# Two heads side by side on TensorE's row and column halves, and two waits moved, in a two-block transformer kernel

## The reference

```python
# first block: 4 heads of 64, keys of this and the previous chunk of 128, bias and mask, a sink in the denominator
logits = einsum('bnqhgd,bnjhd->bnhgqj', qb, kb) * dh ** -0.5
p = exp(logits - m);  probs = p / (sum(p) + exp(sink - m))
out = einsum('bnhgqj,bnjhd->bnqhgd', probs, vb)
# first block: 4 heads of 64 against 256 memory rows, plain softmax
logits = einsum('bshd,bmhd->bhsm', q, mem_k) * dh ** -0.5
# second block: 16 query heads, 4 key heads, over the keys that a top-k of an index score selects
q = rope_partial(rmsnorm(q, q_norm), pos)
logits = where(valid, einsum(q, k_sel) * HEAD_DIM ** -0.5, -inf);  o = einsum(softmax(logits), v_sel)
```

## Time and profile before

| | |
|---|---|
| runs | 1598.68, 1603.06, 1604.56 us; median 1603.06 |
| profiled execution | 1604.89 us, of which 1603.1 are the span of the core |
| PE busy | 1387.6 us, 87% of the span |
| POOL busy | 820.2 us, 51% |
| DVE busy | 640.7 us, 40% |
| ACT busy | 378.0 us, 24% |
| mean granted clock of PE | 0.943 of full |

### The profile page before, as it was taken

One profiled execution on the slowest core, in us unless ns is written; L12 is line 12 of the kernel. 1 busy time (PEld: TensorE's weight loads), 2 busy tenths in 40 slices (PEclk: granted clock), 3 DMA queues, 4 the chain that ended last, 5 costly groups with the idle time before them and its releaser, 6 DMA issues.

```text
span 1603.1 us, 18199 instructions
## 1 busy us (share of the span) xinstructions
PE 1387.6 (87%) x7092; PEld 1024.8 (64%) x7092; DVE 640.7 (40%) x937; ACT 378.0 (24%) x726; POOL 820.2 (51%) x712
## 2 busy tenths in 40 slices
PE   4898889589898589899999999959898499999993
PEld 4777777477676558878778888848776433333331
DVE  3140351424891335463778456661331411111112
ACT  3211142401221235410221544350103011111110
POOL 7678704447758430088888533548792123333320
PEclk9999989799999799999999999989998599999997
DMA  5423200132223020024321212162146069999964
GB/s 187 134 66 105 79 27 27 37 131 80 79 80 105 27 79 1 1 74 136 105 76 57 91 42 67 66 262 100 59 181 266 13 267 379 373 376 377 371 242 173
DMA packets 85235, 216.28 MB, mean 135 GB/s; under 512 B 23508, under 2 KB 32420, under 8 KB 71588
## 3 DMA queue, kind: packets, MB, share of 16 engines
q1 hardware_dynamic: 62076, 199.22, 33.7%
q0 software_dynamic: 13824, 8.44, 1.8%
q10 hardware_dynamic: 9256, 7.51, 1.4%
HBM read 255.99 MB, written 26.22 MB: 176 GB/s over the span
## 4 chain that ended last, share of the span: by engine, by line
PE 47%; PEld 14%; DVE 9%; POOL 6%; issue 6%; DMA 4%; ACT 4%; PEldq 3%; DVEq 3%; ACTq 2%; POOLq 1%; SPq 1%
PE ps L951 10%; PE ps L133 6%; PE ps L134 6%; PE ps L135 6%; PE ps L963 5%; PEld ps L133 5%; PEld ps L134 5%; PEld ps L135 5%; POOL w_lo L484 4%; POOL w_hi L481 3%; PE ps L819 2%; PE ps L723 2%; PE ps L876 2%; PE ps L943 2%; PEldq L596 1%
## 5 line engine op out<-in xcount | busy, mean ns | idle before, releaser
L481 POOL TENSOR_TENSOR w_hi<-stage,unit 128x512 fp32r<-128x512 f32 (+2 forms) x304 | 318.1, 1077 | 476.4 <-PE ps L135 439.9
L484 POOL TENSOR_TENSOR w_lo<-stage,w_hi 128x512 fp32r<-128x512 f32 (+2 forms) x304 | 403.5, 1358 | 10.8
L133 PE MATMUL ps<-hi,w_hi 128*128 128x512 f32 (+1 forms) x600 | 239.0, 398 | 40.5 <-POOL w_lo L484 26.1
L134 PE MATMUL ps<-hi,w_lo 128*128 128x512 f32 (+1 forms) x600 | 236.5, 394 | 0.0
L135 PE MATMUL ps<-lo,w_hi 128*128 128x512 f32 (+1 forms) x600 | 236.0, 393 | 0.0
L133 PE MATMUL ps<-w_hi,hi 128*128 128x512 f32 (+3 forms) x560 | 198.8, 355 | 13.8 <-POOL w_lo L484 6.6
L134 PE MATMUL ps<-w_hi,lo 128*128 128x512 f32 (+3 forms) x560 | 196.8, 351 | 0.0
L135 PE MATMUL ps<-w_lo,hi 128*128 128x512 f32 (+3 forms) x560 | 196.7, 351 | 0.0
L951 PE MATMUL ps<-w_gu,xT 128*64 128x512 f32 x768 | 171.6, 599 | 3.4 <-DMA w_gu<-w_up,over_u 2.0
L133 PEld LDWEIGHTS ps<-hi,w_hi 128*128 128x128 f32 x600 | 115.7, 193 | 70.9 <-issue 27.5
L135 PEld LDWEIGHTS ps<-lo,w_hi 128*128 128x128 f32 x600 | 115.9, 193 | 23.9
(11 more groups left out here) (407 smaller groups left out, 1798.5 us busy)
## 6 DMA issues: line engine op xcount, KB each, us to landing
stage<-w_in SPq DMA_DIRECT2D x84, 512.0 KB, 4.5
w_gu<-w_gate SPq DMA_DIRECT2D x32, 1024.0 KB, 12.4
w_gu<-w_up SPq DMA_DIRECT2D x32, 1024.0 KB, 14.6
w_dn<-w_down SPq DMA_DIRECT2D x32, 1024.0 KB, 10.7
stage<-w_out SPq DMA_DIRECT2D x16, 512.0 KB, 4.6
stage<-w_ssd_branch SPq DMA_DIRECT2D x16, 512.0 KB, 4.7
stage<-w_in SPq DMA_DIRECT2D x20, 256.0 KB, 3.1
stage<-w_attn_branch SPq DMA_DIRECT2D x8, 512.0 KB, 4.2
```

The costliest lines, as they stand in the source:

```text
L133: pe.matmul(out, x[0], w[0], start=first, stop=False)
L134: pe.matmul(out, x[1], w[0], start=False, stop=False)
L481: nc.gpsimd.tensor_tensor(w_hi[:, b, k, 0:n], stage[:, b, k, 0:n], unit[:].broadcast_to([P, n]), ALU.mult)
L484: last = nc.gpsimd.tensor_tensor(w_lo[:, b, k, 0:n], stage[:, b, k, 0:n], w_hi[:, b, k, 0:n].bitcast(F32), ALU.subtract)
```

## The change

1. **Scores.** Queries and keys lie so that head h of an even and an odd number are on the lower and the upper 64 partitions. The four products of a batch use 64 rows each, alternating between the halves (`lanes`). The key tiles need no zeros any more; their memsets go, and ACT writes each key head twice instead.
2. **Values.** The values are the stationary operand (64 columns) and the turned probabilities stream. Even heads go to PSUM partitions 0 to 63, odd heads to 64 to 127, so the result has features on the partitions at once, and the two transposes of the output go. In the second attention a product streams two heads (256 columns).
3. **Denominators.** Since queries now lie on the free axis, the reciprocals must be spread over partitions: four new products per batch (a column broadcast to 64 columns as weights, `ident` streaming) into `p_r`, an ACT copy of `p_r` to `share1` or `share2`, and DVE multiplies `p_v` by it. The reciprocal (`denominators`) is taken one step earlier.
4. **Order.** Per step PE now does the scores of i, the values of i-2, both pairs of transposes of i-1 one after the other, and the spreading product of i-1. There is one step fewer, and the projection in the last two steps comes in three pieces each.
5. **First wait.** DVE signals `sq_ready` right behind the sum of the squares (L1603) instead of behind all rounds, and ACT takes the root before `gate_a(0)`.
6. **Second wait.** SP issues the first two half tiles of `w_ssd_branch` before it waits for `ssd_done`.

```diff
@@ -420,6 +421,7 @@
                 halves(w2, 0, Z2 + 256 * i, 256)
             halves(w2, 0, Z2 + 1536)
+            halves(d["w_ssd_branch_2"][0], 0, 0)
             sp.wait_ge(ssd_done, 1)
             for i in range(7):
                 sp.wait_ge(gate_saved[i], 16)
@@ -433,7 +435,8 @@
             sp.dma_start(xres[:], x1_dram.rearrange("(t p) n -> p t n", p=P)).then_inc(x1_back, 16)
             for r in range(2):
                 for c in range(2):
-                    halves(d["w_ssd_branch_2"][0], 1024 * r, 512 * c)
+                    if (r, c) != (0, 0):
+                        halves(d["w_ssd_branch_2"][0], 1024 * r, 512 * c)
             for c in range(2):
                 halves(d["w_out_2"][0], 0, 512 * c)
             assert tiles[0] == 2 * JOBS
...
@@ -710,22 +713,18 @@
                         if i == batches:
                             pe.wait_ge(s_free, base + batches)
                             chunks = beside()
-                        for _ in range(2):
+                        for _ in range(3):
                             next(chunks)
-                    for half in range(2):
-                        b = i - 2
-                        if 0 <= b < batches:
+                    b = i - 2
+                    if 0 <= b < batches:
+                        for half in range(2):
                             pe.wait_ge(pT_ready[half], base + b + 1)
-                            if base + b > 0 and half == 0:
-                                pe.wait_ge(yt_ready, base + b)
-                            for h in (2 * half, 2 * half + 1):
-                                for kb in range(nkb(b)):
-                                    last = pe.matmul(p_v[:, HD * h:HD * (h + 1)], pT(b)[:, h, P * kb:P * (kb + 1)],
-                                                     values(b, h, kb), start=(kb == 0), stop=(kb == nkb(b) - 1))
-                            if half == 1:
-                                last.then_inc(v_full, 1)
-                        b = i - 1
-                        if 0 <= b < batches:
+                        if base + b > 0:
+                            pe.wait_ge(y_made, base + b)
+                        values(b, p_v).then_inc(v_full, 1)
+                    b = i - 1
+                    if 0 <= b < batches:
+                        for half in range(2):
                             if half == 0:
                                 pe.wait_ge(exp_ready, base + b + 1)
                             if base + b + half > 0:
@@ -735,38 +734,41 @@
                                     last = pe.transpose(p_t[:, h % 2, P * kb:P * (kb + 1)],
                                                         pr(b)[:, h, P * kb:P * (kb + 1)], ident[:])
                             last.then_inc(t_full, 1)
-                    b = i - 3
-                    if 0 <= b < batches:
-                        pe.wait_ge(yt_ready, base + b + 1)
+                        pe.wait_ge(den_ready, base + b + 1)
                         if base + b > 0:
-                            yt_free(b)
-                        for c in range(2):
-                            last = pe.transpose(p_yt[:, P * c:P * (c + 1)], yt[:, b % 2, P * c:P * (c + 1)], ident[:])
-                        last.then_inc(yt_full, 1)
+                            pe.wait_ge(share_ready, base + b)
+                        for h in range(4):
+                            lanes = slice(HD * (h % 2), HD * (h % 2 + 1))
+                            last = pe.matmul(p_r[lanes, P * (h // 2):P * (h // 2 + 1)], sm[:, 5, b % 4, h:h + 1].broadcast_to([P, HD]),
+                                             ident[:], start=True, stop=True)
+                        last.then_inc(r_full, 1)
                 pe.wait_ge(s_free, base + batches)
                 for _ in chunks if beside else ():
                     pass
-                yt_free(batches)
+                pe.wait_ge(y_made, base + batches)
...
@@ -815,16 +817,26 @@
             def scores2(b, s):
                 n, g = query_block(b), b % 4
-                for i in range(4):
-                    last = pe.matmul(s[:, i, 0:P * (n + 1)].rearrange("p (t k) -> p t k", k=P), qT2[:, 4 * (g // 2) + i, P * n:P * (n + 1)],
-                                     kT2[g % 2][g // 2][:, 0:n + 1, :], start=True, stop=True)
+                for h in range(4):
+                    lanes = slice(HD * (h % 2), HD * (h % 2 + 1))
+                    last = pe.matmul(s[:, h, 0:P * (n + 1)], qT2[lanes, 2 * g + h // 2, P * n:P * (n + 1)],
+                                     kT2[g // 2][lanes, g % 2, 0:P * (n + 1)], start=True, stop=True)
+                return last
+
+            def values2(b, out):
+                n, g = query_block(b), b % 4
+                for kb in range(n + 1):
+                    for odd in range(2):
+                        last = pe.matmul(out[HD * odd:HD * (odd + 1), 0:256].rearrange("p (c t) -> p c t", c=2),
+                                         kvt[:, kb, 256 + HD * g:256 + HD * (g + 1)], pT2[:, odd:4:2, P * kb:P * (kb + 1)],
+                                         start=(kb == 0), stop=(kb == n))
                 return last
             pe.wait_ge(kT_ready, 1)
             pe.wait_ge(qT_ready, 2)
...
+            def shares(b, base, dst):
+
+                A.wait_ge(r_full, base + b + 1)
+                if b > 1:
+                    A.wait_ge(y_made, base + b - 1)
+                A.activation(dst[:, b % 2, :], p_r[:, 0:256], ACT.Copy).then_inc(share_ready, 1)
+
...
+            A.wait_ge(sq_ready, 3)
+            A.activation(st[:, 7, 0:64], st[:, 6, 0:64], ACT.Sqrt, scale=1.0 / HD, bias=st[:, 9, 0:1]).then_inc(rms_ready, 1)
             A.wait_ge(x1_saved, 16)
             gate_a(0)
             s = turns.see()
-            for j in range(2):
-                lanes = slice(HD * j, HD * (j + 1))
-                for c in range(2):
-                    last = A.activation(kT2[j][c][lanes], ps[s][lanes, c, :].rearrange("p (t n) -> p t n", t=TT), ACT.Copy)
+            for g in range(4):
+                for odd in range(2):
+                    last = A.activation(kT2[g // 2][HD * odd:HD * (odd + 1), g % 2, :], ps[s][HD * (g % 2):HD * (g % 2 + 1), g // 2, :], ACT.Copy)
             last.then_inc(kT_ready, 1)
             A.drain().then_inc(turn_free[s], 1)
...
             gate_a(1)
-            A.wait_ge(sq_ready, 3)
-            A.activation(st[:, 7, 0:64], st[:, 6, 0:64], ACT.Sqrt, scale=1.0 / HD, bias=st[:, 9, 0:1]).then_inc(rms_ready, 1)
             A.wait_ge(gate_saved[0], 16)
             for c in range(2):
                 s = turns.see()
-
-                for j in range(2):
-                    for odd in range(2):
-                        last = A.activation(qT2[HD * j:HD * (j + 1), 4 * c + odd:4 * c + odd + 3:2, :],
-                                            ps[s][HD * odd:HD * (odd + 1), 2 * j:2 * j + 2, :], ACT.Copy, scale=HD ** -0.5)
-                last.then_inc(qT_ready, 1)
+                A.activation(qT2[:, 4 * c:4 * c + 4, :], ps[s][:], ACT.Copy, scale=HD ** -0.5).then_inc(qT_ready, 1)
                 A.drain().then_inc(turn_free[s], 1)
             s = turns.see()
             A.activation(gate_next[:], ps[s][:], ACT.Tanh, scale=0.5)
             A.drain().then_inc(turn_free[s], 1)
             A.dma_start(gates_dram[1], gate_next[:]).then_inc(gate_saved[1], 16)
-            for i in range(16 + 3):
+            for i in range(16 + 2):
                 if i < 16:
                     softmax(i, 8, P * (query_block(i) + 1), pr2[:, i % 2], pr2[:, i % 2], False)
                 if i == 1:
                     A.wait_ge(gate_saved[1], 16)
                 if 0 <= i - 1 < 16:
                     turned_probabilities(i - 1, 8, P * (query_block(i - 1) + 1), pT2)
-                b = i - 3
+                    shares(i - 1, 8, share2)
+                b = i - 2
                 if b >= 0:
-                    A.wait_ge(yt_full, 8 + b + 1)
+                    A.wait_ge(y_made, 8 + b + 1)
                     n, g = query_block(b), b % 4
                     A.activation(yah[:, 2 * g:2 * g + 2, P * n:P * (n + 1)],
-                                 p_yt[:, 0:256].rearrange("p (c t) -> p c t", c=2), ACT.Copy).then_inc(yT_ready, 1)
+                                 y2[:, b % 2, :].rearrange("p (c t) -> p c t", c=2), ACT.Copy).then_inc(yah_ready, 1)
             def into_conv(n):
...
-            def probabilities_used(b, base, yt, sinks_too):
+            def denominators(b, base, sinks_too):
                 k = b % 4
                 V.wait_ge(exp_ready, base + b + 1)
-                V.wait_ge(v_full, base + b + 1)
                 den = sm[:, 1, k, :]
                 if sinks_too:
                     V.tensor_tensor(den, den, sm[:, 4, k, :], ALU.add)
                     V.drain()
-                V.reciprocal(sm[:, 5, k, :], den)
-                V.drain()
-                V.tensor_tensor(yt[:, b % 2, :].rearrange("p (h d) -> p h d", h=4),
```

(28 more changed lines are left out.)

83 lines of the change are left out of this document (38 added, 45 removed).

## The result

Four executions of the changed kernel took 1572.22, 1574.46, 1577.99 and 1578.34 us, median 1576.22; the four of the kernel before have 1602.06 as their median. The medians lie 25.8 us apart. The ratio on record is 0.9829, with a 95% interval of 0.9801 to 0.9857; of 1602.06 us that is 27.4 us, between 22.9 and 31.9. Forecast were 1575 us, in a range from 1556 to 1591. The profiled execution has 1578.34 us, 26.6 less than that of before.

A forecast was written before the change was run, and what follows sets the result against it. PE, busy 87% of the span, bounds the kernel by its work plus its waits. Gains of 15.0 + 3 + 7 + 0.3 + 2.5 = 27.8 us take 1604.9 to 1577.1, as a median 1575.3; range 1556 to 1591.

The forecast's parts named there:

- Part 1: Early query root: 25.2 us gained at the query wait, less 8.4 new wait and 1.8 half clock: 15.0 us won.
- Part 2, second attention: Second attention: steps at 512 keys fall from 8.9 to 7.9 us; 7 us won, bounds -15 and +25.
- First attention: First attention: memory batches' period falls from 5.56 to 5.2 us; 3 us won, bounds -5 and +8.
- the step that failed: First attention's first four batches: they hang on DVE's sinks and on `lo`, which stay.
- The 0.3 us for shorter read-outs of queries and keys: Read-outs of queries and keys (L1052): 0.3 us shorter.
- Part 3: Early SSD branch weights: projection starts near 1072 instead of 1073.93, clock up earlier; 2.5 us won, bounds 0 and 8.
- the first (POOL not late): Half tile split at 492: POOL isn't late, the early root gives 25 us, total 1565; chance 0.14.
- the third (more late): Half-tile stall grows, next half tile late too, attentions give nothing; early root gives 8, total 1592; chance 0.09.
- The second, PE's own bound: Attentions reach PE's own bound; the second attention gives 25 us, total 1557; chance 0.07.
- The fourth: Attentions: pairs don't overlap in these forms; second loses 15 us, first 5, total 1605; chance 0.03.
- The fifth, the half clock through both attentions: Gaps in each step bring the half clock in both attentions; total 1648, slower; chance 0.03.

The follow-up runs named there:

- Experiment 2: The changed kernel without DVE's two products over the second block's queries, which are then only rotated: ratio 0.9782 to the kernel before.
- root_only: The kernel before with nothing but the early query root (sq_ready signalled behind the sum of squares): 1592.56 us, ratio 0.9920.
- small_readouts: The changed kernel with the second block's queries read out in eight copies of 64 partitions instead of two of 128: 1576.63 us, ratio 0.9821.
- spread_between: The changed kernel with PE's spreading product between the two pairs of transposes instead of behind them: 1568.12 us, ratio 0.9756.
- own_banks: The changed kernel with a bank of its own for each pair of turned probabilities in batches of 256 keys or fewer: 1567.67 us, ratio 0.9748.
- Experiment 4: Two runs on the changed kernel: spreading product between the transpose pairs, 1568.12 us; each pair in its own bank at 256 keys or fewer, 1567.67 us.

## Why the prediction was right

The forecast was 27.8 us against the profiled execution; 26.6 came. The mechanisms of the three parts were the right ones. That the sum comes so close is in part luck, since several terms were missed in both directions and the misses cancel.

- **Part 1, 15.0; measured 15.7.** The wait went, and the new one stands where it was put: 8.16 us against 8.4. The split of the half tile takes 18.8 us from its start against the 19.5 reckoned (481.25 to 500.7). Experiment 2 shows the cause. The projection behind the stop took 23.70 us instead of 22.04, so the restart cost 1.7 us against 1.8. Not seen as a matter of its own: the working put the new read-outs of the queries (1.88 us each) into this part. By root_only 3.6 of the 15.7 us of the trace come with the new layout, and by small_readouts 4.0 with the read-outs alone, though small_readouts is no slower in the whole time.
- **Part 2, second attention, 7; measured 7.25.** The path that bounds the step was the right one: 7.82 us at 512 keys against 7.9. By blocks 32.3, 26.6, 20.6 and 14.7 against 30.6, 27, 21.1 and 15.7; the sums are 94.2 and 94.4. Two terms were mis-sized. The opening two steps took 15.3 us instead of 13.9 and the third 9.1 instead of 7.9, with the second batch's scores at the half clock (3.46 us) and a granted clock of 0.85 over the third step; I had reckoned with less of it. Part of that is the execution's: small_readouts has 14.3 and 7.8 for the same steps. The spreading product issues in 0.59 us (580.87 to 581.46), not 0.45, between its bounds of 0.43 and 0.86: 0.074 us for each of its eight records. In its favour the steps at 256 and 128 keys are 4.82 and 3.4 to 3.6, not 5.05 and 3.7.
- **First attention, 3; measured 2.3.** The memory step fell further than I thought, to 4.71 and not 5.2: the chain over scores, maxima and exponentials lost the scores' half and nothing was added to it, since the copy lies beside the exponentials. But the sliding batches, of which I said that what holds them stays, took 1.3 us more (26.0 instead of 24.7), at a granted clock of 0.74 instead of 0.79. This is no matter of one execution: 25.8 to 26.0 us in all seven traces that have the new attention in this order, 23.7 to 24.7 in the three with the old one. That is the step that failed. The loss arises in the second step, which grew from 6.3 to 8.2 us. Two pieces of new work stand on its path: DVE's sum and reciprocal of the denominators, now ahead of the copy, and PE's spreading product behind the second pair, at the half clock. Before, the copy started 0.07 us after DVE's last step on the maxima:

```profile
202.41 0.16 DVE L1488 TENSOR_SCALAR sm<-sm 128x4 f32<-128x4 f32 x1
202.48 0.41 DVE L1470 COPY pT<-ps 128x256 f32<-128x256 f32 x1
```

In the changed kernel it starts 1.47 us after it, and the spreading product takes 1.05 us more before the next scores at 205.86:

```profile
202.27 0.16 DVE L1491 TENSOR_SCALAR sm<-sm 128x4 f32<-128x4 f32 x1
202.34 1.23 DVE L1460 TENSOR_TENSOR sm<-sm 128x4 f32<-128x4 f32 x1
203.65 0.18 DVE L1462 RECIPROCAL sm<-sm 128x4 f32<-128x4 f32 x1
203.74 0.39 DVE L1473 COPY pT<-ps 128x256 f32<-128x256 f32 x1
```
```profile
204.81 1.12 PE L742 MATMUL ps<-ident,sm 128*64 128x128 f32 x8
```

spread_between, which only moves that product into the wait, brings the stretch back to 24.6. own_banks, which takes the wait for the copy off PE, brings it to 21.8, under the kernel before, since a wait of this kind stood there before the change, too (two of 1.97 and 3.33 us). The 0.3 us for shorter read-outs of queries and keys can't be seen: they lie ahead of the first attention, where this trace lost 1.1 us.

- **Part 3, 2.5; measured 2.6** (0.96 and 1.63), 3.9 by itself with 1.8 to 5.9 as its interval. The split of it was off. Counted from the end of the projection ahead of it, the gates' return is 3.5 us late against 3.3, and the scaled rows are 10.3 us late against 9.7. But the scaling beside POOL took 7.28, not 10, and the products by the gates took 3.4 each instead of 2.29. The start won 1.0, not 1.9. The clock made up the rest: the transposes run at the half clock (6.54 us instead of 3.71) and now stand straight ahead of the projection, whose first 96 products take 22.1 us instead of 23.7. That this total came out at 2.6 is luck as much as reckoning.
- **Not in the sum:** 1.1 us lost ahead of the first attention, 1.3 lost between the branch projection and the gated norm, where one projection ran partly at the half clock (23.6 us instead of 22.0), and 1.0 won at the end.

Of the rivals, the first (POOL not late) and the third (more late) fall with the 8.16 us. The second, PE's own bound, isn't reached by this order. Experiment 4 shows that the order is part of what keeps PE from it: the same work takes 135 us instead of 144 in another order; the rival put it at about 126. The fourth falls because pairs do overlap (1.99 and 1.95 us). The fifth, the half clock through both attentions, didn't come: the granted clock is 0.84 in the second attention's batches of 512 keys and 1.00 behind them, and 0.74 in the sliding batches but 1.00 in the memory batches.

## What to carry to other kernels

When a wait is taken away by starting another engine's work earlier, ask what runs beside it at the new place: here 8.2 of 21.4 us went to a splitter that two long DVE products held up, and a place where the delayed half tile had 4.9 us in hand instead of 1.7 was 5 us cheaper. A faster product exposes what it covered: look for the work that lay in its shadow, and put something else there before counting the gain. Work that an edit adds counts on the path of every stage that shares the code, also of those that the edit wasn't made for. Load weights ahead only so far that their transfers don't stand in the queue before what the next step needs first.

## What the runs showed of the hardware

DVE's products over 4096 elements cost POOL about 9 us of its split wherever they lie: four `w_lo` take 13.73, 13.79 and 14.03 us at three places, 5.03 alone. DVE itself pays little: it takes 4.6 to 5.4 us a product. No run has such a product without POOL beside it; an estimate from the product by the gates over 2048 elements, which takes 2.29 us in the kernel before, is 4.6.

A stop of PE of 2 us leads to the half clock in one execution and not in another (0.60 and 1.00 behind the same wait; seven and three of ten traces), and there each such stretch costs about 1.6 us. Which it will be is not told by the wait alone; what else tells it is open. Stretches that no edit touched differ by as much or more: 86.4 and 90.2 us for the same work at 0.98 and 0.93. So edits of a few microseconds add up only roughly in the whole time, and what one is worth is read from its own stretch of the trace.
